# FFN norm factors formed for a quarter of the tokens per strip, and T4's low parts moved from GpSimd to VectorE, in a one-layer hybrid decoder step

## The chip, the cores and the metric

One core of one Trainium2 chip runs the whole program. The metric is the device time of one execution in microseconds. The kernel before takes 1257.67 us, the median of three runs from 1257.44 to 1259.98.

## What is computed

The reference is one layer over 16 meta tokens, 1,024 prompt tokens and 8 sequences of 4 sample tokens, width 1,024, all in fp32. A mixing part (convolution and gated delta rule) comes first, then the feed-forward part (FFN), which the change is about:

```
h = h + concat([y_a, y_b]) @ w_out
u = relu(rmsnorm(h, norm_ffn) @ w_up)         # w_up is 1024 x 4096
h = h + (u * u) @ w_down
```

`rmsnorm` multiplies each token's row by 1/sqrt(mean of squares + EPS) and each feature by a weight. The kernel multiplies by w_up first and by the token's factor afterwards, since the factor is the same for all outputs of a token.

## The kernel before

Every engine has its own list of instructions, written out by hand in program order; the engines meet by counting semaphores only. An instruction that waits holds all that stand behind it on its engine.

**Numbers.** A matmul operand is split in a high part, a rounding that TensorE takes at full pace, and a low part, the rest. A product is three matmuls for each of four blocks of 128 features: high x high, low x high, high x low (L2328, L2330, L2331, `product`), 12 in all, with 512 token columns each. ScalarE makes the high parts by a copy (L1587 for token operands, `turned_high`; L1595 for weights, `up_set_high`), and GpSimd or VectorE the low parts by a subtraction (L1158 `up_low` on GpSimd for weights; L1165 `turned_low` on GpSimd for token operands T2 and T4; L3192 `turned_low` on VectorE for T3).

**The order of products.** The 4,096 hidden features are taken in 16 pairs of 128. h is held with features in partitions and tokens in columns: 32 sample tokens, then 1,024 prompt tokens (1,056 columns in `hT`, and in `hsq`, the sums of squares). For pair 0 the four blocks of w_up are multiplied with four token operands in eight whole products, here products 1 to 8. From pair 1 on a pair takes seven products instead of eight (Strassen's scheme in Winograd's form), with sums of weight blocks (S1 to S4, made by GpSimd, L1136 to L1152) and of token blocks: B11, B21, B22 are blocks of h, T1 = B11 - B12, T3 = B12 - B22, T2 = B11 - T3, T4 = B21 - T2. A product is named here by pair and token operand. The order on TensorE is products 1 to 8, (1, B11), (1, T1), (1, B21), (1, B22), (1, T3), (1, T2), (1, T4), (2, B11), (2, T1), (2, T3), ... Raw T operands are made by VectorE (`turned_raw`, L3176, L3181, L3186) while products 1 to 8 run. Weight sets have four buffers; the high part of a set waits until the set four places earlier has been used.

**The norm factors.** After product 1 TensorE sums the squares over the partitions with a stationary operand of ones (`sum_h`, L2316): the sum of 1,056 columns is written to all 128 partitions in two matmuls, and after product 2 in a third. VectorE scales and adds EPS (`mean_h`, L3198), ScalarE takes the root of all 1,056 columns (L1639), VectorE takes reciprocals in four parts of 264 columns between its reads of later products (`root_inverse`, L3205).

**The sample tokens** go through the FFN on their own: for each two pairs TensorE runs `sample_up` (L2345, 32 small fp32 matmuls in four strips of 32 output rows, 64 records in the trace), ScalarE copies the result (`sample_copy`, L1604), TensorE transposes it (`sample_turn`, L2354), VectorE applies relu and the norm factor (`sample_scale`, L3217) and ScalarE squares it (`sample_square`, L1608). For pairs 0 and 1 `sample_up(0)` stands behind product 3 and `sample_turn(0)` behind product 7.

**VectorE** reads each finished product out of PSUM (`whole_rows`, L3277 to L3282; `up_rows`, L3241 to L3265; (1, T3) is read twice, L3244 and L3249), later scales rows of u with the factors (`scale_row1`, L3292, `scale_row0`, L3299).

**Loads.** SyncE's queue loads w_up a pair at a time into two buffers (1 MB each); the load for pair 3 waits until the low part of the weight set of (1, T4) is made.

## Time and profile before

| what | us |
|---|---|
| median of three runs | 1257.67 |
| time of the profiled execution | 1257.46 |
| its span in the trace | 1255.7 |
| TensorE (PE) busy | 1237.1, 99% |
| VectorE (DVE) busy | 801.7, 64% |
| GpSimd (POOL) busy | 646.7, 52% |
| ScalarE (ACT) busy | 462.4, 37% |

The span is that of the instructions on the engines; the execution's own time is 1.8 us longer. PE is TensorE's matmuls, PEld its weight loads, SPq the queue of SyncE. A row of a timeline gives start, duration, engine, line, operation, output <- inputs, shapes and, in brackets, how long the engine was idle before and what ended that. A matmul's duration overlaps the next one's; the distance of two starts is what it costs. The FFN begins at 580 us and its first products with w_up fill the stretch to 640 us, which the change touches.

### The profile page before, as it was taken

The page shows a single profiled execution, that of the slowest core. Times are in us where ns is not written, and L with a number is a line of the kernel's source. Part 1 is how long each engine was busy: PE and PEld are TensorE (multiplying, and loading weights), DVE is VectorE, ACT ScalarE, POOL GpSimd, SP SyncE. Part 2 cuts the span into 40 slices and gives each one's busy share as a digit, 9 for nine tenths or more (in the row PEclk, how much of TensorE's full clock was granted, in tenths as well). Part 3 has the DMA queues.
Part 4 walks back from the last instruction along what each step waited for, and adds up shares of the span by engine and source line. Part 5 has one row for each costly group of instructions (what it writes and reads, how often), then busy time and mean ns, then how long its engine had stood idle before and what let it go on. Part 6 is the DMA issues. An engine that isn't in the chain of part 4 may idle for free.

```text
span 1255.7 us, 20503 instructions
## 1 busy us (share of the span) xinstructions
PE 1237.1 (99%) x7950; PEld 1090.9 (87%) x7950; DVE 801.7 (64%) x1283; ACT 462.4 (37%) x810; POOL 646.7 (52%) x503
## 2 busy tenths in 40 slices
PE   7999999999999999999999999999999999999997
PEld 6899999899999999998778888888887888878897
DVE  6465899535564766655987685565666667556456
ACT  6565654311222222224333333333434533333312
POOL 2332120112111212213889898888789989887811
PEclk9999999999999999999999999999999999999999
DMA  6132672843323322231145353444655442541003
GB/s 205 43 85 71 176 211 72 220 123 93 93 68 85 103 68 84 79 92 52 44 158 170 121 165 136 141 143 151 226 168 202 168 140 96 201 135 68 17 10 129
DMA packets 164706, 151.07 MB, mean 120 GB/s; under 512 B 21095, under 2 KB 141315, under 8 KB 161922
## 3 DMA queue, kind: packets, MB, share of 16 engines
q1 hardware_dynamic: 141634, 136.88, 34.4%
q10 hardware_dynamic: 22976, 12.88, 3.7%
q8 instruction: 64, 1.05, 0.3%
q14 instruction: 32, 0.26, 0.1%
HBM read 103.25 MB, written 46.49 MB: 119 GB/s over the span
## 4 chain that ended last, share of the span: by engine, by line
PE 95%; DVE 2%; POOL 1%; issue 1%; DMA 1%; ACT 1%; SPq 0%; POOLq 0%; DVEq 0%; ACTq 0%
PE banks L2328 15%; PE banks L2330 15%; PE banks L2331 15%; PE banks L1792 11%; PE banks L1794 11%; PE banks L1793 11%; PE banks L2359 1%; PE banks L2345 1%; PE banks L2441 1%; PE banks L2442 1%; PE banks L2443 1%; PE banks L2262 1%; PE banks L1978 1%; DMA w_raw<-in_w_in 1%; PE banks L1971 1%
## 5 line engine op out<-in xcount | busy, mean ns | idle before, releaser
L1792 PE MATMUL banks<-xn_high,w_high 128*128 128x384 f32 (+1 forms) x672 | 227.2, 338 | 1.0 <-DVE xn_low L2565 0.9
L1794 PE MATMUL banks<-xn_high,w_low 128*128 128x384 f32 (+1 forms) x672 | 218.9, 326 | 0.0
L1793 PE MATMUL banks<-xn_low,w_high 128*128 128x384 f32 (+1 forms) x672 | 218.8, 326 | 0.0
L1002 POOL TENSOR_TENSOR w_low<-w_raw,w_high 128x1024 fp32r<-128x1024 f32 x30 | 76.8, 2559 | 230.9 <-ACT w_high L1280 230.9
L3333 DVE TENSOR_TENSOR hT<-hT,banks 128x512 f32<-128x512 f32 x148 | 98.3, 684 | 109.2 <-PE banks L2331 108.4
L1792 PEld LDWEIGHTS banks<-xn_high,w_high 128*128 128x128 f32 x672 | 127.1, 189 | 6.8 <-issue 3.6
L2328 PE MATMUL banks<-op_high,set_high 128*128 128x512 f32 x336 | 131.6, 392 | 0.0
L2330 PE MATMUL banks<-op_low,set_high 128*128 128x512 f32 x336 | 130.8, 389 | 0.0
L2331 PE MATMUL banks<-op_high,set_low 128*128 128x512 f32 x336 | 130.7, 389 | 0.0
L1793 PEld LDWEIGHTS banks<-xn_low,w_high 128*128 128x128 f32 x672 | 127.4, 190 | 0.0
L1794 PEld LDWEIGHTS banks<-xn_high,w_low 128*128 128x128 f32 x672 | 127.0, 189 | 0.0
L1158 POOL TENSOR_TENSOR set_low<-w_up_sum,set_high 128x512 fp32r<-128x512 f32 x59 | 97.4, 1656 | 28.2 <-ACT set_high L1595 28.2
L2328 PE MATMUL banks<-up_high_T,set_high 128*128 128x512 f32 x248 | 97.8, 395 | 1.8 <-POOL up_low_T L1165 1.4
L2330 PE MATMUL banks<-up_low_T,set_high 128*128 128x512 f32 x248 | 96.6, 390 | 0.0
L2331 PE MATMUL banks<-up_high_T,set_low 128*128 128x512 f32 x248 | 96.5, 389 | 0.0
L1158 POOL TENSOR_TENSOR set_low<-w_up_raw,set_high 128x512 fp32r<-128x512 f32 x49 | 77.1, 1574 | 36.7 <-ACT set_high L1595 36.6
L2328 PE MATMUL banks<-up_high_B,set_high 128*128 128x512 f32 x204 | 80.8, 396 | 0.4 <-POOL set_low L1158 0.4
L2330 PE MATMUL banks<-up_low_B,set_high 128*128 128x512 f32 x204 | 79.5, 390 | 0.0
L2331 PE MATMUL banks<-up_high_B,set_low 128*128 128x512 f32 x204 | 79.4, 389 | 0.0
L1595 ACT ACTIVATE set_high<-w_up_sum 128x512 fp32r<-128x512 f32 x59 | 37.3, 632 | 112.0 <-PE banks L2331 88.3
L2328 PEld LDWEIGHTS banks<-op_high,set_high 128*128 128x128 f32 x336 | 63.1, 188 | 15.1 <-issue 2.2
L1233 POOL TENSOR_TENSOR set_low<-w_down,set_high 128x512 fp32r<-128x512 f32 x36 | 67.2, 1873 | 16.8 <-ACT set_high L1704 16.7
(419 smaller groups left out, 2839.9 us busy)
## 6 DMA issues: line engine op xcount, KB each, us to landing
op_raw<-ops_kept SPq DMA_DIRECT2D x21, 1024.0 KB, 5.0
w_up_raw<-in_w_up SPq DMA_DIRECT2D x16, 1024.0 KB, 6.5
w_raw<-in_w_in SPq DMA_DIRECT2D x28, 512.0 KB, 4.4
ops_kept<-u_rows SPq DMA_DIRECT2D x28, 512.0 KB, 2.7
ops_kept<-u_T SPq DMA_DIRECT2D x42, 256.0 KB, 2.4
w_down_half<-in_w_down SPq DMA_DIRECT2D x3, 2048.0 KB, 9.0
w_down<-in_w_down SPq DMA_DIRECT2D x24, 256.0 KB, 4.2
w_raw<-in_w_out SPq DMA_DIRECT2D x8, 512.0 KB, 3.8
```

The costliest lines, as they stand in the source:

```text
L1002: pool.tensor_tensor(w_l[n % 2][:, :, :], w_raw[n % 2][:, :, :], w_h[n % 2][:, :, :].bitcast(F32), ALU.subtract).then_inc(w_low, 1)
L1158: pool.tensor_tensor(set_l[s % 4][:, :, :], up_source_at(s), set_h[s % 4][:, :, :].bitcast(F32), ALU.subtract).then_inc(w_low, 1)
L1233: pool.tensor_tensor(down_set(b, set_l, s), down_source(b, pair, PRODUCTS[x][0]), down_set(b, set_h, s).bitcast(F32), ALU.subtract).then_i ...
L1595: act.activation(set_h[s % 4][:, :, :], up_source(c, name), ACT.Copy).then_inc(w_high, 1)
L1792: pe.matmul(bank[:, 0:w], w_h[n % 2][:, k, :], hi[:, c0:c0 + w], start=(k == first), stop=False)
L1793: pe.matmul(bank[:, 0:w], w_h[n % 2][:, k, :], lo[:, c0:c0 + w], start=False, stop=False)
L1794: ins = pe.matmul(bank[:, 0:w], w_l[n % 2][:, k, :], hi[:, c0:c0 + w], start=False, stop=(k == last))
L1971: ins = pe.matmul(ps[5][0:c, c * h:c * h + c], kf[:, h, o:o + c], kf[:, h, o:o + c], start=True, stop=True)
L2328: pe.matmul(bank, high[:, j, :], op_high[:, j, :], start=(j == 0 and not begun), stop=False, skip_group_check=True)
L2330: pe.matmul(bank, high[:, j, :], op_low[:, j, :], start=False, stop=False, skip_group_check=True)
L2331: ins = pe.matmul(bank, low[:, j, :], op_high[:, j, :], start=False, stop=(j == n - 1), skip_group_check=True)
L3333: dve.tensor_tensor(hc, hc, both, ALU.add if sign > 0 else ALU.subtract).then_inc(acc_read_dve, 1)
```

## The change

The sums of squares are now formed by four matmuls, each over a quarter of the columns (264) and into its own strip of 32 partitions of one PSUM bank, so that [128, 264] holds all 1,056 columns. VectorE's `mean_h`, ScalarE's root and VectorE's reciprocal run once over 264 columns. `spread_h` on TensorE then writes each strip to all 128 partitions, in four banks (it sums 32 equal rows, for which `mean_h` corrects by a factor), and four ScalarE copies bring the factors back to `hsq`. `sample_up(0)` moves behind product 7 and waits for those copies, `sample_turn(0)` behind (1, T1). The low parts of T4 move from GpSimd to VectorE, and `sample_scale(0)` on VectorE moves from behind the read of (1, B21) to behind the read of (1, T3).

```diff
         A22_LOADED = [W_UP[-1] + 16 * (2 * parts_to(b) - n) for b, (_, n) in enumerate(BLOCKS)]
         A12_LOADED = [W_UP[-1] + 16 * 2 * parts_to(b) for b in range(len(BLOCKS))]
 
-        UP_HIGHS, ROOT_HIGH = {"T1": 0, "T3": (21, 22, 24, 25), "T2": (26, 27, 28, 29), "T4": (30, 31, 32, 33)}, 23
-        FIRST_HIGH, FIRST_LOW = 33, 20
-        UP_LOWS = {"B11": 7, "T1": 8, "B21": 15, "B22": 16, "T3": 20}
+        UP_HIGHS, ROOT_HIGH = {"T3": (22, 23, 24, 25), "T2": (26, 27, 28, 29), "T4": (30, 31, 32, 33)}, 21
+        FIRST_HIGH, FIRST_LOW = 33, 24
+        SPREAD_BANKS = (1, 3, 5, 7)
+        UP_LOWS = {"B11": 7, "T1": 8, "B21": 15, "B22": 16, "T3": 20, "T4": 24}
 
         def last_index(n):
             return sum(has_last(m) for m in range(n))
...
             up_low(1, 2)
             turned_low("T2", 3)
             up_low(1, 3)
-            turned_low("T4", 0)
-            turned_low("T4", 1)
             up_low(1, 5)
-            turned_low("T4", 2)
-            turned_low("T4", 3)
             for c in range(2, UP_PAIRS):
                 up_sum(c)
                 up_low(c, 0)
...
             last_half_scaled(2)
             last_half_scaled(3)
             up_set_high(0, 6)
+            act.wait_ge(rstd_mid, 1)
+            act.activation(hsq[:, 0:QUARTER], hsq[:, 0:QUARTER], ACT.Sqrt).then_inc(high_s, 1)
             turned_high("T3", 0)
             turned_high("T3", 1)
-            act.wait_ge(rstd_mid, 3)
-            act.activation(hsq[:, 0:KEPT], hsq[:, 0:KEPT], ACT.Sqrt).then_inc(high_s, 1)
+            act.wait_ge(h_sum, 2)
+            for j in range(4):
+                act.activation(hsq[:, QUARTER * j:QUARTER * j + QUARTER], ps[SPREAD_BANKS[j]][:, 0:QUARTER],
+                               ACT.Copy).then_inc(rstd_mid, 1)
+            up_set_high(1, 0)
             sample_copy(0)
-            up_set_high(1, 0)
             turned_high("T3", 2)
             turned_high("T3", 3)
             up_set_high(1, 1)
...
                     bank_free(f, g)
                     dense_part(N_IN + f, g, mixed, range(KT))
 
-            def sum_h(g):
-
-                c0, w = KEPT_GROUPS[g]
+            def sum_h():
+
                 pe.wait_ge(h_sq, 3 * N_OUT)
-                if g == 0:
-                    pe.wait_ge(x_slice_kept, 3 * N_OUT)
-                if g == 2:
-                    pe.wait_ge(rstd_mid, 1)
-                pe.matmul(ps[6 + g % 2][:, 0:w], one[:, 0:1].to_broadcast([P, P]), hsq[:, c0:c0 + w], start=True,
-                          stop=True).then_inc(h_sum, 1)
+                pe.wait_ge(x_slice_kept, 3 * N_OUT)
+                for j in range(4):
+                    ins = pe.matmul(ps[6][QUAD * j:QUAD * j + QUAD, 0:QUARTER], one[:, 0:1].to_broadcast([P, QUAD]),
+                                    hsq[:, QUARTER * j:QUARTER * j + QUARTER], start=True, stop=True)
+                ins.then_inc(h_sum, 1)
+
+            def spread_h():
+
+                pe.wait_ge(rstd_mid, 2)
+                for j in range(4):
+                    rows_ = slice(QUAD * j, QUAD * j + QUAD)
+                    ins = pe.matmul(ps[SPREAD_BANKS[j]][:, 0:QUARTER], one[rows_, 0:1].to_broadcast([QUAD, P]),
+                                    hsq[rows_, 0:QUARTER], start=True, stop=True)
+                ins.then_inc(h_sum, 1)
 
             def product(u, s, high, low, op_high, op_low, begun):
 
                 pe.wait_ge(w_low, set_made(s))
                 if u == U_UNIT[0, 4]:
-                    pe.wait_ge(rstd_mid, 3)
+                    pe.wait_ge(rstd_mid, 1)
                 else:
                     pe.wait_ge(acc_read_dve, banks_read_before(u))
                 n, bank = high.shape[1], unit_bank(u)
...
 
                 if m == 0:
                     pe.wait_ge(smp_dve, 2)
+                    pe.wait_ge(rstd_mid, 6)
                 pe.wait_ge(w_load[0], W_UP[2 * m])
                 pe.wait_ge(w_load[1], W_UP[2 * m + 1])
                 if m >= 2:
...
 
             def up(c, x):
                 u, s, name = U_UNIT[c, x], U_SET[c, x], PRODUCTS[x][1]
-                if c == 1 and name == "T3":
+                if c == 1 and name in ("T3", "T4"):
                     pe.wait_ge(low_s, UP_LOWS[name])
-                if c == 1 and name in ("T2", "T4"):
-                    pe.wait_ge(turned_low_s, 4 if name == "T2" else 8)
+                if c == 1 and name == "T2":
+                    pe.wait_ge(turned_low_s, 4)
                 product(u, s, set_h[s % 4], set_l[s % 4], up_h[name], up_l[name], x >= 4 and (c, x) != (1, 6))
 
             def down(b, x, pair):
...
             for i in range(len(WHOLE)):
                 up_whole(i)
                 if i == 0:
-                    sum_h(0)
-                    sum_h(1)
-                if i == 1:
-                    sum_h(2)
-                if i == 2:
+                    sum_h()
+                if i == 4:
+                    spread_h()
+                if i == 6:
                     sample_up(0)
-                if i == 6:
-                    sample_turn(0)
             for c, x in U_SEQ[len(WHOLE):]:
                 up(c, x)
                 if c % 2 == 0 and x == 1:
                     sample_up(c // 2)
+                if (c, x) == (1, 1):
+                    sample_turn(0)
                 if c % 2 == 0 and x == 3:
                     sample_turn(c // 2)
                 if (c, x) == (UP_PAIRS - 1, 3):
...
                 dve.tensor_tensor(up_l[name][:, j, :], up_raw[name][:, j, :], up_h[name][:, j, :].bitcast(F32),
                                   ALU.subtract).then_inc(low_s, 1)
 
-            def mean_h(g):
-                c0, w = KEPT_GROUPS[g]
-                dve.wait_ge(h_sum, g + 1)
-                dve.tensor_scalar(hsq[:, c0:c0 + w], ps[6 + g % 2][:, 0:w], 1.0 / D, EPS, ALU.mult,
+            def mean_h():
+
+                dve.wait_ge(h_sum, 1)
+                dve.tensor_scalar(hsq[:, 0:QUARTER], ps[6][:, 0:QUARTER], float(QUAD ** 2) / D, QUAD ** 2 * EPS, ALU.mult,
                                   ALU.add).then_inc(rstd_mid, 1)
 
-            def root_inverse(i):
-
-                cols = slice(QUARTER * i, QUARTER * i + QUARTER)
+            def root_inverse():
+
                 dve.wait_ge(high_s, ROOT_HIGH)
-                link(dve.reciprocal(hsq[:, cols], hsq[:, cols]))
+                dve.reciprocal(hsq[:, 0:QUARTER], hsq[:, 0:QUARTER]).then_inc(rstd_mid, 1)
 
             def sample_rows():
...
             def sample_scale(m):
 
                 dve.wait_ge(smp_turned, m + 1)
+                if m == 0:
+                    dve.wait_ge(rstd_mid, 6)
                 dve.scalar_tensor_tensor(out=sample_quad(m),
                                          in0=ps[3][:, P * (m % 2):P * (m % 2) + P].rearrange("p (j c) -> p j c", c=NS),
                                          scalar=0.0, in1=hsq[:, 0:NS].unsqueeze(1).to_broadcast([P, 4, NS]), op0=ALU.max,
...
             whole_rows(0)
             sample_rows()
             half_low("B22", N_OUT - 1, 1, 16)
-            mean_h(0)
-            mean_h(1)
+            mean_h()
             turned_raw("T3", 0)
             whole_rows(1)
-            mean_h(2)
             turned_raw("T3", 1)
             whole_rows(2)
+            root_inverse()
             turned_raw("T3", 2)
             turned_raw("T3", 3)
             whole_rows(3)
...
             turned_raw("T4", 3)
             turned_low("T3", 3)
             up_rows(1, 1)
-            root_inverse(0)
+            turned_low("T4", 0)
+            turned_low("T4", 1)
             up_rows(1, 4)
-            root_inverse(1)
+            turned_low("T4", 2)
+            up_rows(1, 6)
+            turned_low("T4", 3)
+            up_rows(1, 2)
             sample_scale(0)
-            up_rows(1, 6)
-            root_inverse(2)
-            up_rows(1, 2)
-            root_inverse(3)
             up_rows(1, 3)
             scale_row1(0)
             up_rows(1, 5)
```

On ScalarE (`u_sample_tok` is the copy of sample_up's result, `up_raw_T_75` and `up_high_T_63` are T3, `set_high_119` here the set of (1, B11), `set_high_120` that of (1, T1), `up_high_T_64` T2). Before:

```order
L1587 ACTIVATE up_high_T_63<-up_raw_T_75 128x512 [waits turned_s] x2
L1639 ACT_TABLE_LOAD
L1639 ACTIVATE h_squares<-h_squares 128x1056 [waits rstd_mid]
L1604 ACTIVATE u_sample_tok_256<-banks 128x128 [waits smp_strips]
L1595 ACTIVATE set_high_119<-w_up_raw_230 128x512 [waits acc_done,w_load1]
L1587 ACTIVATE up_high_T_63<-up_raw_T_75 128x512 [waits turned_s] x2
L1595 ACTIVATE set_high_120<-w_up_sum_232 128x512 [waits acc_done,s_made,w_load1]
L1587 ACTIVATE up_high_T_64<-up_raw_T_74 128x512 [waits turned_s] x4
```

With the change:

```order
L1634 ACT_TABLE_LOAD
L1634 ACTIVATE h_squares<-h_squares 128x264 [waits rstd_mid]
L1584 ACTIVATE up_high_T_63<-up_raw_T_75 128x512 [waits turned_s] x2
L1639 ACTIVATE h_squares<-banks 128x264 [waits h_sum]
L1639 ACTIVATE h_squares<-banks 128x264 x3
L1592 ACTIVATE set_high_119<-w_up_raw_230 128x512 [waits acc_done,w_load1]
L1601 ACTIVATE u_sample_tok_256<-banks 128x128 [waits smp_strips]
L1584 ACTIVATE up_high_T_63<-up_raw_T_75 128x512 [waits turned_s] x2
L1592 ACTIVATE set_high_120<-w_up_sum_232 128x512 [waits acc_done,s_made,w_load1]
L1584 ACTIVATE up_high_T_64<-up_raw_T_74 128x512 [waits turned_s] x4
```

The root has moved ahead of T3's first high parts, the four copies behind them, and the copy for the sample behind set (1, B11); behind it stand the same high parts as before.

On VectorE, from the read of (1, T1) to that of (1, T2) (`u_rows_249` takes the products of pair 1, `up_low_T_72` is T4, `u_sample` the sample's scaling). Before:

```order
L3244 TENSOR_TENSOR u_rows_249<-u_rows_249,banks 128x512 [waits acc_read_dve,acc_done]
L3205 RECIPROCAL h_squares<-h_squares 128x264 [waits high_s]
L3256 COPY u_rows_249<-banks 128x512 [waits acc_done,dve_step]
L3205 RECIPROCAL h_squares<-h_squares 128x264 [waits high_s]
L3217 SCALAR_TENSOR_TENSOR u_sample_253<-banks,h_squares 128x128 [waits smp_turned,dve_step]
L3265 COPY u_rows_249<-banks 128x512 [waits acc_done]
L3205 RECIPROCAL h_squares<-h_squares 128x264 [waits high_s]
L3244 TENSOR_TENSOR u_rows_249<-u_rows_249,banks 128x512 [waits acc_read_dve,acc_done,dve_step]
L3249 TENSOR_TENSOR u_rows_249<-u_rows_249,banks 128x512 [waits acc_read_dve]
L3205 RECIPROCAL h_squares<-h_squares 128x264 [waits high_s]
L3252 TENSOR_TENSOR u_rows_249<-u_rows_249,banks 128x512 [waits acc_read_dve,acc_done,dve_step]
```

With the change:

```order
L3253 TENSOR_TENSOR u_rows_249<-u_rows_249,banks 128x512 [waits acc_read_dve,acc_done]
L3200 TENSOR_TENSOR up_low_T_72<-up_raw_T_76,up_high_T_65 128x512 [waits high_s] x2
L3265 COPY u_rows_249<-banks 128x512 [waits acc_done]
L3200 TENSOR_TENSOR up_low_T_72<-up_raw_T_76,up_high_T_65 128x512 [waits high_s]
L3274 COPY u_rows_249<-banks 128x512 [waits acc_done]
L3200 TENSOR_TENSOR up_low_T_72<-up_raw_T_76,up_high_T_65 128x512 [waits high_s]
L3253 TENSOR_TENSOR u_rows_249<-u_rows_249,banks 128x512 [waits acc_read_dve,acc_done]
L3258 TENSOR_TENSOR u_rows_249<-u_rows_249,banks 128x512 [waits acc_read_dve]
L3226 SCALAR_TENSOR_TENSOR u_sample_253<-banks,h_squares 128x128 [waits rstd_mid,smp_turned]
L3261 TENSOR_TENSOR u_rows_249<-u_rows_249,banks 128x512 [waits acc_read_dve,acc_done]
```

Four reciprocals have left, four low parts of T4 have come, and the sample's scaling stands three reads later, behind both reads of (1, T3).

## Rows read from the trace of the kernel before

**Rows 1.** Table of stages: stage, length, then PE, PEld, DVE, ACT, POOL busy, clock, DMA share, GB/s.

```profile
616.00:640.00 24.00, 21.80 (x149) 16.87 (x148) 20.09 (x16) 7.10 (x12) 24.00 (x17) 1.00 0.29 101
```

**Rows 2.** Timeline of PE, 616 to 632 us: start, us, engine, line, operation, shapes, count, idle.

```profile
617.03 0.39 PE L2328 MATMUL banks<-up_high_T,set_high 128*128 128x512 f32 x1
...
622.25 0.39 PE L2331 MATMUL banks<-up_high_T,set_low 128*128 128x512 f32 x1
624.00 0.50 PE L2328 MATMUL banks<-up_high_T,set_high 128*128 128x512 f32 x1 [1.37 <-POOL up_low_T L1165]
...
627.47 0.50 PE L2328 MATMUL banks<-up_high_B,set_high 128*128 128x512 f32 x1 [0.41 <-POOL set_low L1158]
...
630.94 0.50 PE L2328 MATMUL banks<-up_high_T,set_high 128*128 128x512 f32 x1 [0.42 <-POOL set_low L1158]
```

**Rows 3.** Timeline of PE, 583 to 593 us, around the sums and sample_up(0).

```profile
583.00 1.29 PE L2316 MATMUL banks<-h_squares,one 128*128 128x288 f32 x4
...
584.36 0.39 PE L2330 MATMUL banks<-up_low_T,set_high 128*128 128x512 f32 x1
...
586.90 0.81 PE L2316 MATMUL banks<-h_squares,one 128*128 128x384 f32 x2
...
587.77 0.39 PE L2330 MATMUL banks<-up_low_B,set_high 128*128 128x512 f32 x1
...
592.62 0.40 PE L2330 MATMUL banks<-up_low_B,set_high 128*128 128x512 f32 x1
```

**Rows 4.** Timeline of PE, 150 us: four strip sums of 304 columns (8 records).

```profile
149.97 0.34 PE L1794 MATMUL banks<-xn_high,w_low 128*128 128x384 f32 x1
150.24 0.70 PE L1912 MATMUL banks<-squares,pick 128*32 128x304 f32 x8
150.87 0.50 PE L1948 MATMUL banks<-g_spread,g_pick 128*128 128x256 f32 x2
```

**Rows 5.** Timeline of ACT, 592 and 618 us.

```profile
592.42 0.28 ACT L1604 ACTIVATE u_sample_tok<-banks 128x128 f32<-128x128 f32 x1
...
593.11 1.14 ACT L1587 ACTIVATE up_high_T<-up_raw_T 128x512 fp32r<-128x512 f32 x2
...
617.91 0.31 ACT L1608 ACTIVATE u_sample<-u_sample 128x128 f32<-128x128 f32 x1 [5.40 <-DVE u_sample L3217]
618.13 1.14 ACT L1595 ACTIVATE set_high<-w_up_raw 128x512 fp32r<-128x512 f32 x2
```

**Rows 6.** Timeline of POOL, 608 to 631 us.

```profile
608.81 5.14 POOL L1165 TENSOR_TENSOR up_low_T<-up_raw_T,up_high_T 128x512 fp32r<-128x512 f32 x3
...
623.88 1.31 POOL L1136 TENSOR_TENSOR w_up_sum<-w_up_raw 128x512 f32<-128x512 f32 x1
625.12 2.30 POOL L1158 TENSOR_TENSOR set_low<-w_up_raw,set_high 128x512 fp32r<-128x512 f32 x1
...
628.62 2.27 POOL L1158 TENSOR_TENSOR set_low<-w_up_sum,set_high 128x512 fp32r<-128x512 f32 x1
```

**Rows 7.** Timeline of DVE, 613 to 622 us.

```profile
615.76 1.79 DVE L3205 RECIPROCAL h_squares<-h_squares 128x264 f32<-128x264 f32 x1
617.59 0.29 DVE L3217 SCALAR_TENSOR_TENSOR u_sample<-banks,h_squares 128x128 f32<-128x128 f32 x1
...
620.22 0.69 DVE L3244 TENSOR_TENSOR u_rows<-u_rows,banks 128x512 f32<-128x512 f32 x1
620.83 0.68 DVE L3249 TENSOR_TENSOR u_rows<-u_rows,banks 128x512 f32<-128x512 f32 x1
```

**Rows 8.** Timeline of SP, 621 us, and the page on the DMA issues.

```profile
621.51 0.37 SPq L860 DMA_DIRECT2D w_up_raw<-in_w_up  x1
...
w_up_raw<-in_w_up SPq DMA_DIRECT2D x16, 1024.0 KB, 6.5
```

**Rows 9.** Timeline of PE, 17 us, near the start of the kernel.

```profile
17.18 0.46 PE L1794 MATMUL banks<-xn_high,w_low 128*128 128x304 f32 x1
17.44 0.46 PE L1792 MATMUL banks<-xn_high,w_high 128*128 128x304 f32 x1
```

## The prediction

> **What bounds the kernel.** A product is named by its weight pair and the token operand it uses, as (1, T3). I read the table of stages first, then TensorE's timeline, then the other engines' timelines over the same microseconds. In the stage from 616 to 640 us TensorE is busy for 21.80 of 24 us at a granted clock of 1.00 [rows 1]. Before and after that stage it hardly pauses, so the end of the kernel moves by whatever TensorE loses or wins here. TensorE's timeline shows where it loses [rows 2]. A product is 12 matmuls of 512 columns, 0.23 us apart, so 2.72 us. The last matmul of (1, T2) starts at 622.25, and (1, T4) starts at 624.00 instead of 622.48: the wait is put down to GpSimd's last low part of T4. (2, B11) starts at 627.47 and (2, T1) at 630.94, each 0.4 us after it could, both for a low weight set from GpSimd. With the slower first matmul after each pause (0.35 instead of 0.23) these waits cost 3.0 us: two products from 622.48 on would have let (2, T1) start at 627.9 instead of 630.94. GpSimd is the engine behind, and the diff takes four of its instructions away. The question is whether that queue really ends earlier.
>
> **The change, part by part.**
>
> *Sums on TensorE.* The first two sums take from 583.00 to 584.13 (the second matmul of the next product starts at 584.36, 0.23 after its first would have), 1.13 us; the third from 586.90 to 587.54, 0.64 us [rows 3]. Removed: 1.77 us for 1,056 columns. Added: four sums of 264 columns into four strips of 32 output rows. The nearest rows are four such strip sums of 304 columns in the mixing part: from 150.15 (0.17 after the start at 149.97) to 150.87, 0.72 us [rows 4]. By rows 3 a column costs 1.77/1,056 us, so 304 take 0.51 and 264 take 0.44; 0.72 less 0.07, plus 0.1 for the slower restart: I take 0.75. The spread is four matmuls that each read one strip of 32 input rows and write all 128 output rows to banks of their own. No row shows input strips side by side; the lower bound is the 0.72 of rows 4, the upper the 1.77 of rows 3 (one after another). I take 0.75, because different strips and different banks leave nothing that they share. Net on TensorE: 0.75 + 0.75 - 1.77 = **-0.3 us** (+0.8 at the upper bound).
>
> *Roots and reciprocals.* VectorE loses four reciprocals of 1.79 us and gets one, and four low parts of T4 instead; ScalarE's root shrinks from 1,056 to 264 columns and four copies of PSUM are added. TensorE waits for none of it: the reciprocal is done some 2.5 us after the third product (its row is read in 0.7, then 1.79), and the spread comes only after the fifth, 5.4 us after it. This part costs and gives nothing.
>
> *The sample's products are moved, and ScalarE's queue is not.* This is the term that decides. TensorE issues sample_up(0) after product 7 instead of after product 3, since it now waits for the spread norms. ScalarE still has sample_copy(0), which waits for it, ahead of the last two high parts of T3, of set (1, T1), of all four of T2 and so on. Before, sample_up(0) ended at 592.39 (0.23 before the start at 592.62) and the copy started at 592.42 [rows 3, 5]. Now it ends four products later, less the saving on the sums, plus the spread: 592.39 + 4 x 2.72 - (1.77 - 0.75) + 0.75 = 603.0 us. ScalarE then does the copy (0.2), two high parts (1.14) and the high part of set (1, T1) (0.6): 605.0 us [rows 5]. GpSimd can begin the low part of that set at 605.0, not earlier.
>
> From there GpSimd has nine instructions up to the end of low set (1, T3) (low (1, T1), S2, low (1, B21), S4, low (1, B22), three low parts of T2, low (1, T3)), and one wait of 0.7 us, since S4 goes to ScalarE for its high part first. Their price has two ends in this trace: 1.31 where VectorE is not reading two SBUF operands, 1.71 (5.14 for three) where it is [rows 6]. Sum: 605.0 + 0.7 + 9 x 1.31 = 617.5 at the least, and with 9 x 1.71 it is 621.1 at the most. I take 1.66, near the upper end, because VectorE has the raw and low parts of T3 and T4 in just these microseconds, now four low parts of T4 more: **620.6 us**.
>
> The Trainium skill, "GPSIMD Engine Reference", section "Key points", says that GpSimd shares its SBUF interfaces with VectorE and is disturbed by VectorE's instructions with two SBUF inputs. That speaks against moving T4's subtractions to VectorE: by the rule alone all nine cost the upper price and the kernel ends at 1261.7; if it did not hold, the lower price and 1258.1. The trace agrees as far as it goes (1.71 beside such instructions, 1.31 without).
>
> TensorE is ready for (1, T3) at 617.03 - 0.3 = 616.75 [rows 2]. It waits **3.9 us**, and starts 3.6 us later than before.
>
> *sample_scale(0) moved behind (1, T3) on VectorE.* ScalarE's sample_square(0) waits for it, and the high part of set (1, T4) stands behind that square (before: square at 617.91, high part at 618.13 [rows 5]). Now: product (1, T3) ends; VectorE begins to read it 0.2 us later (a matmul lasts 0.39 and the next starts after 0.23 [rows 2]), reads it twice (0.61 each), scales (0.29), ScalarE squares (0.22 until the next begins) and makes the high part (0.6) [rows 5, 7]. With the handovers that is 2.6 us after the product's end at 620.6 + 2.8 = 623.4: 626.0. GpSimd's low set then takes 1.3 to 1.5: (1, T4) starts at 627.5, against 624.00: again **+3.5 us**. So the four instructions taken from GpSimd give nothing: the wait for T4's low part is replaced by a wait for T4's weight set, 1.4 us after (1, T2) ends at 626.1.
>
> *After that* GpSimd does S1, low (2, B11), S3, low (2, T1) as before, from 623.88 to 630.89, 7.0 us [rows 6]; now from 627.5 to 634.5. (2, T1) starts at 634.5 against 630.94. From here TensorE runs without a pause, as before, and nothing gives the time back.
>
> *DMA.* The load of weight pair 3 waits for low set (1, T4): issued at 621.51 before [rows 8], now 6 us later, 627.5; with 6.5 to land it is there at 634.0, and its first reader, sample_up(1), comes after (2, T1), at 634.5 + 2.7 = 637.2. Hidden, with 3 us to spare.
>
> **Sum.** +3.5 us. The profiled execution has a span of 1255.7 and a time of 1257.46, so 1259.2 and 1261.0; the median of the runs is 0.2 above it: **1261.2 us**. A measurement of this kernel tells from no change what is beyond 0.2%, 2.5 us: 1255.2 to 1260.2 counts as the same.
>
> **Rivals.**
>
> 1. *GpSimd catches up in part.* If its nine instructions cost 1.31 to 1.5 us, (1, T3) starts at 617.5 to 619.2, 0.5 to 2.2 later than before, and everything behind it too: 1258.1 to 1259.9. For it: VectorE's copies out of PSUM and its pauses do not slow GpSimd. Against: the three at 608.8 averaged 1.71 with less beside them. Chance 0.16.
>
> 2. *The clock falls in the new pause.* The longest pause of TensorE after its start is now 1.4 us, and the clock stays at its upper level, 2.4 GHz. A pause of 3.9 us is not in this trace. What the lower level costs is: at 17 us the matmuls of 304 columns start 0.25 apart, which is 1.2 GHz [rows 9]; by that 512 columns take 0.43 instead of 0.23, 2.4 us more for a product. If (1, T3) runs so, the end is +5.9, 1263.6; with (1, T2) too, 1 us more, since most of that is hidden by the wait for T4's set: 1264.6. Chance 0.12. The Trainium skill, "TensorE: Matmul & The Clock Gate", section "Loop structure matters more than you think", warns that waits between bursts of matmuls bring the clock down to half; only the rows at the start speak to it here.
>
> 3. *The spread's strips run one after another*: 1.77 instead of 0.75, sample_up(0) ends 1.0 later, and with it the whole chain: 1262.2. Chance 0.06.
>
> 4. *Faster.* GpSimd is relieved of four instructions of at least 1.3 us, and TensorE's 3.0 us of waits and the 0.3 of the sums come back: 1254.4. It decides itself at two points: low set (1, T3) must be done by 616.75, and the high part of set (1, T4) must be made by 620. Against: the second hangs on sample_scale(0), which is now queued behind (1, T3), and even with the first point met the chain from that product's end gives 619.5 + 2.6 + 1.4 = 623.6, 0.4 better than before, not 3. Chance 0.04.
>
> **How the numbers follow.** My forecast has 0.62, its own range 1260.4 to 1262.0. It and rivals 2 and 3 are slower by over 0.2% but for a few per cent of the forecast: 0.76. Same: rival 1 and those few, 0.20. Faster: 0.04. The range from 1258.8 to 1263.7 leaves out the faster case, the lower half of rival 1 and half of rival 2, 0.18.
>
> **What would show it.** Right: in the changed profile ScalarE idles until about 603 us for sample_up(0); GpSimd idles until about 605; TensorE pauses nearly 4 us before (1, T3), put down to a low weight set, not to a low part of T; a second pause of 1.4 us before (1, T4), again for a weight set, with ScalarE's square waiting for VectorE just ahead. Wrong: (1, T3) starts before 619; or matmuls behind the pause stand 0.43 apart; or the spread takes over 1.5 us.

## The result and the profile after

The changed kernel takes **1261.04 us**, the median of 20 runs (1258.28 to 1264.57); the kernel before, run beside it on the same chip, 1257.68 us (20 runs, 1255.54 to 1259.98). The ratio is 1.0034, 95% interval 1.0028 to 1.004: slower by 3.4 us. The profiled execution has a span of 1259.1 us and a time of 1260.87 us.

The table of stages and TensorE's timeline of the changed kernel, with the columns of [rows 1] and [rows 2]; the product's lines are now L2336, L2338 and L2339:

```profile
616.00:640.00 24.00, 19.01 (x128) 14.49 (x129) 11.92 (x13) 6.46 (x11) 19.32 (x13) 0.93 0.21 67
616.00:619.00 3.00, 0.00 (x0) 0.00 (x0) 1.81 (x3) 0.00 (x0) 3.00 (x3) 1.00 0.00 0
619.00:622.00 3.00, 2.97 (x7) 2.42 (x8) 0.00 (x0) 0.00 (x0) 2.40 (x2) 0.51 0.00 0
```

```profile
619.03 0.71 PE L2336 MATMUL banks<-up_high_T,set_high 128*128 128x512 f32 x1 [3.13 <-issue]
619.54 0.63 PE L2338 MATMUL banks<-up_low_T,set_high 128*128 128x512 f32 x1
619.97 0.63 PE L2339 MATMUL banks<-up_high_T,set_low 128*128 128x512 f32 x1
...
622.52 0.40 PE L2339 MATMUL banks<-up_high_T,set_low 128*128 128x512 f32 x1
622.76 0.40 PE L2336 MATMUL banks<-up_high_T,set_high 128*128 128x512 f32 x1
...
627.45 0.47 PE L2336 MATMUL banks<-up_high_T,set_high 128*128 128x512 f32 x1 [1.12 <-issue]
...
630.87 0.50 PE L2336 MATMUL banks<-up_high_B,set_high 128*128 128x512 f32 x1 [0.42 <-POOL set_low L1159]
...
634.34 0.50 PE L2336 MATMUL banks<-up_high_T,set_high 128*128 128x512 f32 x1 [0.41 <-POOL set_low L1159]
```

TensorE is busy for 19.01 of the 24 us instead of 21.80. It stands still for 3.13 us before (1, T3), and then the clock is down: the matmuls stand 0.43 us apart until 622.52, at a granted clock of 0.51, the lower of its two levels, 1.2 GHz. A pause of 1.12 us before (1, T4) follows, and the two pauses of 0.4 us before (2, B11) and (2, T1) are still there. "issue" as releaser means that no semaphore event of the trace falls on the end of the wait; what ended it shows on the other engines. ScalarE and GpSimd, answering to [rows 5] and [rows 6]:

```profile
595.55 0.66 ACT L1592 ACTIVATE set_high<-w_up_raw 128x512 fp32r<-128x512 f32 x1
602.00 0.28 ACT L1601 ACTIVATE u_sample_tok<-banks 128x128 f32<-128x128 f32 x1 [5.79 <-PE banks L2354]
602.18 1.14 ACT L1584 ACTIVATE up_high_T<-up_raw_T 128x512 fp32r<-128x512 f32 x2
603.22 0.62 ACT L1592 ACTIVATE set_high<-w_up_sum 128x512 fp32r<-128x512 f32 x1
...
625.17 0.31 ACT L1605 ACTIVATE u_sample<-u_sample 128x128 f32<-128x128 f32 x1 [12.49 <-DVE u_sample L3226]
625.39 1.14 ACT L1592 ACTIVATE set_high<-w_up_raw 128x512 fp32r<-128x512 f32 x2
```

```profile
603.92 1.30 POOL L1159 TENSOR_TENSOR set_low<-w_up_sum,set_high 128x512 fp32r<-128x512 f32 x1 [5.10 <-ACT set_high L1592]
...
612.15 5.11 POOL L1166 TENSOR_TENSOR up_low_T<-up_raw_T,up_high_T 128x512 fp32r<-128x512 f32 x3
617.23 1.70 POOL L1159 TENSOR_TENSOR set_low<-w_up_sum,set_high 128x512 fp32r<-128x512 f32 x1
...
626.08 1.27 POOL L1159 TENSOR_TENSOR set_low<-w_up_raw,set_high 128x512 fp32r<-128x512 f32 x1 [4.68 <-ACT set_high L1592]
```

ScalarE idles 5.79 us for sample_up(0), GpSimd 5.10 us behind it for the high part of set (1, T1); the low set of (1, T3) ends at 618.93, and TensorE starts 0.1 later. After (1, T3), ScalarE's square ends an idle time of 12.49 us, GpSimd waits 4.68 us for the high part behind it, and then TensorE gets set (1, T4).

The sums, answering to [rows 3]:

```profile
581.96 0.66 PE L2314 MATMUL banks<-h_squares,one 128*32 128x264 f32 x8
...
593.66 0.73 PE L2323 MATMUL banks<-h_squares,one 32*128 32x264 f32 x8
```

The first sum starts at 581.96 instead of 583.00. This 1.04 us does not come from the change, but from the start of the kernel, which the change does not touch. In this execution the matmuls of 304 columns stand 0.14 us apart from 15.00 on, where those of [rows 9], at 17 us, are still 0.25 apart:

```profile
14.54 0.46 PE L1793 MATMUL banks<-xn_high,w_high 128*128 128x304 f32 x1
14.79 0.37 PE L1794 MATMUL banks<-xn_low,w_high 128*128 128x304 f32 x1
15.00 0.30 PE L1795 MATMUL banks<-xn_high,w_low 128*128 128x304 f32 x1
15.14 0.30 PE L1793 MATMUL banks<-xn_high,w_high 128*128 128x304 f32 x1
```

I therefore compare stretches by one distance: from the start of the first sum to the start of sample_up(1), which stands behind (2, T1). It is 633.89 - 583.00 = 50.89 us before, and 637.28 - 581.96 = 55.32 after: **+4.43**, of which the luck at the start hides 1.04; the other 3.4 us are what the spans show.

### The profile page after: what moved, and what is told of

It is laid out like the page before. It is cut to its first block, busy times and chain, and to the rows that moved or that the text cites. A ratio compares the mean times of both kernels' runs of the same rounds, so it can differ in the third digit from the quotient of the medians.

```text
span 1259.1 us, 20517 instructions
## 1 busy us (share of the span) xinstructions
PE 1237.4 (98%) x7960; PEld 1089.8 (87%) x7960; DVE 798.0 (63%) x1282; ACT 461.7 (37%) x814; POOL 640.7 (51%) x499
## 4 chain that ended last, share of the span: by engine, by line
PE 92%; issue 3%; DVE 2%; POOL 2%; ACT 1%; DMA 1%; SPq 0%; ACTq 0%; POOLq 0%; DVEq 0%
PE banks L2336 14%; PE banks L2339 14%; PE banks L2338 14%; PE banks L1793 11%; PE banks L1795 11%; PE banks L1794 11%; PE banks L2368 1%; PE banks L2452 1%; PE banks L2450 1%; PE banks L2451 1%; PE banks L2354 1%; PE banks L2263 1%; PE banks L1979 1%; POOL set_low L1159 1%; DMA w_raw<-in_w_in 1%
## 5 line engine op out<-in xcount | busy, mean ns | idle before, releaser
L2336 PE MATMUL banks<-op_high,set_high 128*128 128x512 f32 x336 | 131.6, 392 | 0.0
L2338 PE MATMUL banks<-op_low,set_high 128*128 128x512 f32 x336 | 130.8, 389 | 0.0
L2339 PE MATMUL banks<-op_high,set_low 128*128 128x512 f32 x336 | 130.7, 389 | 0.0
L2336 PE MATMUL banks<-up_high_T,set_high 128*128 128x512 f32 x248 | 98.5, 397 | 4.7 <-issue 4.3
L2338 PE MATMUL banks<-up_low_T,set_high 128*128 128x512 f32 x248 | 97.3, 392 | 0.0
L2339 PE MATMUL banks<-up_high_T,set_low 128*128 128x512 f32 x248 | 97.0, 391 | 0.0
L2336 PE MATMUL banks<-up_high_B,set_high 128*128 128x512 f32 x204 | 80.5, 395 | 0.4 <-POOL set_low L1159 0.4
L2338 PE MATMUL banks<-up_low_B,set_high 128*128 128x512 f32 x204 | 79.5, 390 | 0.0
L2339 PE MATMUL banks<-up_high_B,set_low 128*128 128x512 f32 x204 | 79.4, 389 | 0.0
L2336 PEld LDWEIGHTS banks<-op_high,set_high 128*128 128x128 f32 x336 | 63.1, 188 | 15.0 <-issue 2.2
```

The source lines that it names most:

```text
L2336: pe.matmul(bank, high[:, j, :], op_high[:, j, :], start=(j == 0 and not begun), stop=False, skip_group_check=True)
L2338: pe.matmul(bank, high[:, j, :], op_low[:, j, :], start=False, stop=False, skip_group_check=True)
L2339: ins = pe.matmul(bank, low[:, j, :], op_high[:, j, :], start=False, stop=(j == n - 1), skip_group_check=True)
```

## The experiments

"Stretch" is that distance, as the difference to the 50.89 of before. The kernels E1 to E4 ran on one chip beside 35 runs of before (median 1257.85), E5 to E8 on another beside 29 (1258.44), E9 and E10 on a third beside 21 (1256.36), E11 and E12 on a fourth beside 19 (1260.07).

| kernel | stretch | waits of TensorE in it | median | ratio, 95% |
|---|---|---|---|---|
| before | 0 | 1.37, 0.41, 0.42 | | |
| changed, its profile | +4.43 | 3.13, 1.12, 0.42, 0.41 | 1261.04 | 1.0034, 1.0028 to 1.004 |
| E1 copy later | -0.55 | 1.12, 0.42, 0.46 | 1257.7 | 1.0002, 0.9993 to 1.0011 |
| E2 square later | 0.0 | 3.13 | 1258.99 | 1.001, 1.0 to 1.002 |
| E3 both later | -3.42 | none | 1254.68 | 0.9974, 0.9965 to 0.9983 |
| E4 T4 alone | +0.77 | 2.13 | 1258.38 | 1.0008, 1.0 to 1.0017 |
| E5 pause filled | +2.89 | 0.46, 1.12, 0.42, 0.41 | 1259.31 | 1.0006, 0.9992 to 1.002 |
| E6 changed, T4 back | +4.60 | 1.35, 4.50 | 1262.41 | 1.0023, 1.0009 to 1.0038 |
| E7 E3, T4 back | -0.23 | 1.35, 0.46, 0.42 | 1257.56 | 0.9981, 0.9967 to 0.9995 |
| E8 changed again | +2.86 | 3.13, 1.12, 0.45, 0.46 | 1261.03, one run | |
| E9 T4 alone, gaps | -1.68 | 0.92 | 1255.28 | 0.9991, 0.9982 to 1.0 |
| E10 as E3 | -3.41 | none | 1254.24 | 0.9978, 0.9969 to 0.9986 |
| E11 T4 alone, late | -2.13 | 0.78 | 1255.34 | 0.9969, 0.9954 to 0.9983 |
| E12 as E3 | -3.42 | none | 1254.54 | 0.9964, 0.9952 to 0.9976 |

**E1.** The changed kernel, with the sample's copy behind T4's second high part on ScalarE:

```diff
             up_set_high(1, 0)
-            sample_copy(0)
             turned_high("T3", 2)
...
             turned_high("T4", 1)
+            sample_copy(0)
             up_set_high(1, 6)
```

> The changed kernel with one line moved: ScalarE's sample_copy(0) stands behind the second high part of T4, ahead of set (1, B22), instead of ahead of T3's last high parts. Theory (the copy that waits for the moved sample_up(0) holds ScalarE and with it GpSimd's chain): GpSimd does low set (1, T1) right after S3, TensorE has no pause before (1, T3), no matmul there stands 0.43 apart, and only the wait before (1, T4) for its weight set stays, 1.4 us. (2, T1) starts about where it does in the kernel before: ratio to before 0.9995 to 1.000, 1257.2 us. Rival (GpSimd's nine instructions, slowed by VectorE's T4 subtractions, are late by themselves): a pause of over 1 us before (1, T3) stays, 1259 or more.

The pause before (1, T3) is gone; (1, T4) still starts 1.12 us late, and the stretch is 2.86 + 0.55 = 3.4 us shorter than that of the changed kernel (E8). Without that one line's place on ScalarE's list there is no first pause; how long the pause is depends on T4's move too, as E6 shows below. The median came out 0.5 us above the one expected.

**E2.** The changed kernel, with the square behind the second high set of pair 2 instead of ahead of the high part of set (1, T4):

```diff
-            sample_square(0)
             up_set_high(1, 5)
...
             for x in range(3):
                 up_set_high(2, x)
+                if x == 1:
+                    sample_square(0)
```

> The changed kernel with the other line moved: ScalarE's sample_square(0) stands behind the high part of set (2, T1) instead of ahead of set (1, T4). Theory (the second wait, before (1, T4), comes from sample_scale(0) behind (1, T3) and the square ahead of the high part): the pause of 3 us before (1, T3) stays with its slow matmuls, the pause before (1, T4) is gone, GpSimd starts S1 of pair 2 some 3 us earlier, the waits at (2, B11) and (2, T1) shrink to nothing: 3 us less than the changed kernel, 1257.5 to 1258.5. Rival (T4's low parts, now on VectorE, are what (1, T4) waits for): it stays at 1261.

The pause before (1, T3) stays, and nothing behind it waits any more, (2, B11) and (2, T1) included: the square's place costs 2.86 us, more than the 1.12 of its own pause, since GpSimd no longer begins pair 2 late. The median, 1258.99, is 0.5 us above the range expected and 1.1 above before, though the stretch is that of before. In the profiled execution the clock stayed up in the pause; in seven of the twelve runs the mean granted clock was lower than in any run of before on that chip (see E8).

**E3.** Both moves.

> Both lines moved. Theory: what the two moves of sample_up(0) and sample_scale(0) did through ScalarE's order is undone, and what remains is the relief of GpSimd by four instructions and 0.3 us less of sums on TensorE: no pause before (1, T3), (1, T4), (2, B11), at most 0.5 us before (2, T1): 3.3 us faster than before, 1254.2. Rival (relief is given back elsewhere, in ScalarE or VectorE): within 1 us of before.

TensorE never waits. Its windows, columns as in [rows 1]:

```profile
610.00:614.00 4.00, 4.00 (x20) 3.26 (x19) 4.00 (x4) 1.62 (x3) 4.00 (x4) 1.00 0.00 0
614.00:618.00 4.00, 4.00 (x19) 3.31 (x18) 4.00 (x5) 0.63 (x1) 4.00 (x3) 1.00 0.00 0
618.00:622.00 4.00, 4.00 (x19) 3.33 (x18) 3.66 (x6) 0.63 (x1) 4.00 (x4) 1.00 0.00 0
622.00:626.00 4.00, 4.00 (x20) 3.30 (x19) 2.77 (x3) 1.46 (x3) 4.00 (x4) 1.00 0.81 237
```

GpSimd begins low set (1, T1) at 600.84, 16.84 us behind the first sum (584.00 here), and not 21.96 behind it as in the changed kernel:

```profile
600.84 1.75 POOL L1159 TENSOR_TENSOR set_low<-w_up_sum,set_high 128x512 fp32r<-128x512 f32 x1
602.55 1.73 POOL L1141 TENSOR_TENSOR w_up_sum<-w_up_sum,w_up_raw 128x512 f32<-128x512 f32 x1
...
614.68 1.74 POOL L1159 TENSOR_TENSOR set_low<-w_up_sum,set_high 128x512 fp32r<-128x512 f32 x1
```

The time is below both kernels. **E10 and E12** are the same kernel on two more chips:

> The changed kernel with both moves on ScalarE's list (sample_copy(0) behind T4's second high part, sample_square(0) behind the second high set of pair 2), run once more on another occasion and beside the kernel that keeps the norm as it was. If the order of ScalarE's list is what the change lacked: no wait of TensorE in the stretch, 3 to 3.5 us less than before, ratio 0.9973 or so again. If the first result leant on its chip or on luck with the clock: a ratio over 0.9985.

> The changed kernel with both moves on ScalarE's list, on the same chip and in the same rounds as the kernel with the norm kept, so that the two can be compared within one occasion. Theory A: 1 us or more faster than the kernel with the norm kept. Theory B: within 0.5 us of it.

The stretch agrees to 0.01 us on all three chips, and each interval lies wholly below 1.

**E4.** The kernel before, with only T4's low parts moved to VectorE, between its four reciprocals:

```diff
             up_rows(1, 1)
+            turned_low("T4", 0)
+            turned_low("T4", 1)
             root_inverse(0)
             up_rows(1, 4)
-            root_inverse(1)
+            turned_low("T4", 2)
             sample_scale(0)
+            root_inverse(1)
             up_rows(1, 6)
+            turned_low("T4", 3)
             root_inverse(2)
```

> The kernel before with T4's low parts on VectorE, among its four reciprocals, and everything of the norm as it was. Theory: VectorE then has 4 x 0.65 to 1.7 us more in front of (1, T4), with four reciprocals of 1.79 in the same queue; (1, T4) starts about when it did, at 624, its wait now for VectorE or none, but GpSimd is ahead afterwards and the waits at (2, B11) and (2, T1) go: 1.0 to 1.5 us faster, 1256.3. Rival (VectorE cannot take them beside four whole reciprocals): (1, T4) waits for VectorE's low part and later, 1258 to 1260.

VectorE is late in GpSimd's place. A reciprocal at 619.63 holds up the read of (1, B22), whose bank (1, T2) needs. VectorE first, then TensorE:

```profile
619.63 1.79 DVE L3201 RECIPROCAL h_squares<-h_squares 128x264 f32<-128x264 f32 x1
621.46 0.69 DVE L3261 COPY u_rows<-banks 128x512 f32<-128x512 f32 x1
```

```profile
622.29 0.77 PE L2324 MATMUL banks<-up_high_T,set_high 128*128 128x512 f32 x1 [2.13 <-DVE u_rows L3261]
622.86 0.63 PE L2326 MATMUL banks<-up_low_T,set_high 128*128 128x512 f32 x1
623.28 0.63 PE L2327 MATMUL banks<-up_high_T,set_low 128*128 128x512 f32 x1
```

Here too the clock fell, after a pause of 2.13 us: (1, T2) takes 4.37 us to the next product's start instead of some 2.8, so an estimate of the stretch without the fall is 0.77 - 1.55 = -0.8. The gain expected, 1.0 to 1.5 us in the median, did not come; as the rival had it, VectorE could not take the four beside four reciprocals, but it was late with a read and not with a low part.

**E6 and E7.** T4's low parts back on GpSimd, in the changed kernel (E6) and in E3 (E7):

```diff
             up_low(1, 3)
+            turned_low("T4", 0)
+            turned_low("T4", 1)
             up_low(1, 5)
+            turned_low("T4", 2)
+            turned_low("T4", 3)
```

> The changed kernel with T4's low parts back on GpSimd, in their old places; everything of the norm and the sample's moves stays. Theory: (1, T3) starts 0.5 to 1.8 us earlier, since GpSimd's instructions before it stand beside fewer VectorE instructions with two SBUF inputs, but GpSimd has four more in front of the end: (1, T4) waits for the last low part of T4 again and starts 1 to 1.5 us later than in the changed kernel; in all 0.3 to 1 us more, 1261.5. Rival (moving T4 to VectorE is what made the changed kernel slow): 1258 or less.

> The version with both lines moved, but T4's low parts back on GpSimd: the norm part of the change alone, without its harm through ScalarE's order. Theory: the norm's part gives only the 0.3 us of the sums less 0.1, since the old waits for T4's low part at (1, T4), and for the sets of (2, B11) and (2, T1), are all back: within 0.5 us of the kernel before, 1257.5. Rival (the reciprocals taken from VectorE are worth something by themselves, GpSimd being less disturbed or banks free earlier): 1 us or more faster than before.

E6 has the longest stretch and the highest median, 0.9 us above the one expected (its ratio, 1.0023, stands beside a before of 1258.44 on that chip). GpSimd begins low set (1, T1) 21.96 us behind the first sum, as in the changed kernel, but is through with its nine instructions up to low set (1, T3) sooner:

```profile
612.67 3.79 POOL L1166 TENSOR_TENSOR up_low_T<-up_raw_T,up_high_T 128x512 fp32r<-128x512 f32 x3
616.41 1.26 POOL L1159 TENSOR_TENSOR set_low<-w_up_sum,set_high 128x512 fp32r<-128x512 f32 x1
```

These four take 5.05 us, where they take 5.11 + 1.70 = 6.81 in the changed kernel. (1, T3) starts 35.29 us behind the first sum instead of 37.07, and TensorE waits 1.35 us before it instead of 3.13. The only difference is T4's subtractions. So 1.78 us of the first pause is what they cost GpSimd when they run on VectorE, and 1.35 us is left when the copy is late and they are not there. Behind that, GpSimd has four more instructions, and TensorE waits 4.50 us for the last low part of T4 (granted clock 0.77 from 626 to 630, so the clock fell here too). (1, T4) starts 45.48 us behind the first sum, against 43.89 in E8: counted to that point, T4's move is worth 1.6 us in the late chain.

E7 has the waits of [rows 2] again and only the sums' gain: the norm's change alone is worth 0.2 us in the stretch, as expected. Its ratio, 0.9981, would be 2.4 us; the trace shows nothing of that size, and the runs of before on that chip scatter from 1255.6 to 1263.7 us, so I go by the stretch. The ratios of E11 and E12 lean on a high median of before in the same way.

**E9 and E11.** Is the norm's change needed at all? The kernel before with T4's low parts on VectorE and other places for the reciprocals. E9 fills VectorE's gap of 2.8 us before the fourth whole product's read with the first one and puts the second behind T3's second low part; E11 puts the second to fourth behind T4's last low part and the two reads after it. In both, T4's first two low parts stand behind the read of (1, T1) and the third behind that of (1, B21). The two edits in one, without the lines that are taken out:

```diff
             turned_raw("T3", 3)
+            root_inverse(0)
             whole_rows(3)
...
             turned_low("T3", 1)
+            root_inverse(1)       # E9 only
             whole_rows(7)
...
             turned_low("T4", 3)
+            root_inverse(1)       # E11; root_inverse(2) in E9
             up_rows(1, 2)
+            root_inverse(2)       # E11; root_inverse(3) in E9
             up_rows(1, 3)
+            root_inverse(3)       # E11 only
```

> The kernel before with T4's low parts on VectorE and the norm left as it was, but with two of the four reciprocals moved into earlier gaps of VectorE: the first behind the last raw part of T3, the second behind T3's second low part; sample_scale(0) behind T4's third low part. It asks whether the quartered norm is needed at all. Theory A (T4's move and the norm's change need each other because VectorE has no room for four reciprocals and four low parts): VectorE comes late with a read or a low part in this order too, TensorE waits 1 us or more for VectorE, and the time is that of the kernel before or more, 1257.5 to 1259. Theory B (only the order mattered, the room is there in the gaps): no wait of TensorE for VectorE between (1, T3) and (2, T1), sample_up(1) comes 3.4 to 3.7 us earlier, as with the good order of the changed kernel, 1254.0 to 1254.9. In between, 1255 to 1257: the early reciprocals hold up T3's low parts or GpSimd a little.

> As the run before it with the norm kept as it was and T4's low parts on VectorE, but the second reciprocal, behind which the read of (1, B11) came late there (TensorE waited 0.92 us before (1, B21)), stands behind T4's last low part, and the third and fourth one read later each. VectorE has its gap of 2.8 us filled by the first reciprocal only. Theory A (VectorE has no room for four reciprocals in this stretch wherever they stand; the quartered norm is needed for the full gain): a new wait for VectorE turns up, at (1, T4) or at pair 2, and sample_up(1) comes at most 2 us earlier than before, 1255.5 or more. Theory B (it was the place alone): no wait, sample_up(1) 3.0 us earlier (the whole of the waits of before, without the 0.1 to 0.4 of the sums), 1254.5 to 1255.1; then the norm's change is worth only its 0.1 to 0.4 us of sums.

Each leaves one wait for a late read of VectorE, 0.92 us before (1, B21) in E9 and 0.78 us before (2, T1) in E11:

```profile
629.48 0.47 PE L2324 MATMUL banks<-up_high_T,set_high 128*128 128x512 f32 x1 [0.78 <-DVE u_rows L3259]
```

Both stretches are shorter than that of before, though E9's ratio reaches 1.0 and E11's leans on a slow before. E10 and E12, beside them, are quicker still: stretches of -3.4 against -1.7 and -2.1, medians 1.0 and 0.8 us lower. Both results lie between what the two theories expected: a wait for VectorE is there (theory A), but part of the gain comes without the norm's change (theory B). In the two orders tried VectorE had no room for all four reciprocals; that no order has it is not shown.

**E5 and E8.** E8 is the changed kernel once more. E5 puts 12 matmuls of 512 columns into the pause, behind (1, B22), that write a bank nobody reads before it is overwritten:

```diff
+                if (c, x) == (1, 6):
+                    for j in range(12):
+                        pe.matmul(ps[7][:, :], up_h["B22"][:, 0, 0:P], up_h["B22"][:, j % 4, :], start=True, stop=True)
```

> The changed kernel with 12 more matmuls of 512 columns into a PSUM bank that nobody reads, between (1, B22) and (1, T3), so that TensorE works through 2.7 of the 3.1 us in which it waits; the rest is unchanged. Theory (in the changed kernel's profile the clock fell to its lower level in the pause and cost 1.5 us on (1, T3)): (1, T3) starts at the same distance from the FFN's begin, its matmuls stand 0.23 apart, (1, T4) and all behind it come up to 1.5 us earlier than in that profile; in the median over runs 0.5 to 1.5 us less than the changed kernel, 1259.6 to 1260.5, and its runs scatter less. Rival (the slow matmuls have another cause, such as GpSimd or loads): they stay slow and the time is 1261 or, with the added work, more.

> The changed kernel once more, one look with a profile. Theory: the pause of 3.1 us before (1, T3) is there again to 0.1 us, and whether the clock falls in it is open, since it did here and not in the same pause with the square moved; if it doesn't, the stretch is 1.5 us shorter. Rival (the fall belongs to the changed kernel): the matmuls of (1, T3) stand 0.43 apart again.

The stretch of E8 is +2.86, not +4.43, with the same pauses. Its windows show why:

```profile
616.00:619.00 3.00, 1.65 (x8) 1.03 (x6) 3.00 (x5) 0.00 (x0) 3.00 (x3) 1.00 0.00 0
619.00:622.00 3.00, 1.22 (x5) 1.05 (x6) 0.56 (x1) 0.00 (x0) 3.00 (x4) 1.00 0.00 0
622.00:625.00 3.00, 3.00 (x15) 2.48 (x14) 1.20 (x2) 0.00 (x0) 1.17 (x1) 1.00 0.00 0
```

The clock stayed at its upper level, 2.4 GHz. So the changed kernel's two late lines leave it 2.86 us behind before in an execution in which the clock stays up, and 1.57 us further behind in one in which it falls in the pause.

How often it falls there in the timed runs is not known; their mean granted clocks give a hint. A mean of 0.996 or less was found in this many runs:

| chip | kernels without a pause over 1.4 us | kernels with one (its length) |
|---|---|---|
| result | | changed 8 of 20 (3.13) |
| E1 to E4 | before 0 of 35, E1 0 of 12, E3 1 of 12 | E2 7 of 12 (3.13), E4 7 of 11 (2.13) |
| E5 to E8 | before 10 of 29, E5 0 of 12, E7 0 of 12 | E6 8 of 12 (4.50), E8 0 of 1 (3.13) |
| E9, E10 | before 0 of 21, E9 2 of 11, E10 1 of 11 | |
| E11, E12 | before 8 of 19, E11 4 of 9, E12 1 of 11 | |

The eight of the changed kernel are its slowest runs, 1261.61 to 1264.57, and on the chip of E1 to E4 the low means go with the long pauses. But the mean does not single out this fall. The profiled executions of the changed kernel and of E4 have the fall in the stretch and a mean of 0.997; that of E11 has 0.996 and no fall in the stretch, but one at 57 us and one at 1248. E8 has a fall at 57 us too, where the change is not yet at work:

```profile
57.00:58.00 1.00, 1.00 (x5) 1.00 (x5) 0.66 (x3) 0.97 (x2) 0.20 (x2) 0.50 0.00 0
```

Falls like these may be what lowers the mean of before on two of the chips; no trace of such a run of before was taken.

E5's stretch of +2.89 is that of E8, so filling the pause could only gain in executions where the clock falls. None of its 12 runs was at 0.996 or less, and its median, 1259.31, lies 0.3 us below the range expected, but its ratio, 1.0006 with an interval of 0.003, can't be set against that of the changed kernel, which was timed on another chip: what the filling saves on the median stays open.

## Why the prediction was right

Times are moved by +1.04 (changed kernel) or by -0.71 (E8), so that the first sum starts at 583.00.

- *Sums.* Forecast 0.75; measured 581.87 to 582.65, 0.78. Spread: forecast 0.75, measured 0.85 (593.58 to 594.43). Four strips of 32 input rows do run beside each other, and **rival 3 falls**. Net -0.14 instead of -0.3, of no account.
- *sample_up(0) ends* at 603.0 (forecast 603.0); *low set (1, T1) starts* at 604.96 (605.0). This was the step that decides, and E1 shows that without it there is no first pause.
- *GpSimd's nine instructions* took 14.2 us, 1.58 each; I took 1.66. The low set of (1, T3) was done at 619.97 instead of 620.6, and TensorE paused 3.13 instead of 3.9 us. This is the term that was mis-sized, by 0.7 us: the first two instructions cost the lower price, 1.30. VectorE is idle beside the first until 604.9; beside most of the second it makes a raw part from two SBUF inputs, and there it is VectorE's instruction that is slow, 1.50 instead of 0.74. **Rival 1**, at 1.5 or less, is out, though by little: in E6, without T4's subtractions on VectorE, the nine took 12.4 us, 1.38 each, which lies in its range. The rule of the Trainium skill that I weighed ("GPSIMD Engine Reference", "Key points": GpSimd and VectorE share SBUF interfaces) would have had all nine at 1.71. The trace agrees with it for the other seven, which took 1.5 to 1.75, and E6 agrees with what I took from it against T4's move (1.78 us); the second instruction, at 1.30, does not agree. The upper price that I read, 1.71, is also not the highest of [rows 6]: a low set there takes 2.30. None of the nine met that price.
- *sample_scale(0) behind (1, T3)*: from that product's end to the start of (1, T4) 4.0 us, forecast 4.1. In E8 (1, T4) starts at 626.9, forecast 627.5, and the 0.6 between them is GpSimd's. E2 shows the square as the cause.
- *Pair 2*: GpSimd needs 7.0 us, as forecast. (2, T1) is at 633.8 in E8, forecast 634.5, so the forecast of +3.5 was **+2.86** without the clock.
- *The load* of pair 3 was issued at 628.4 (forecast 627.5), and sample_up(1) did not wait for it.
- **Rival 2**, the clock falling in the pause, came true in the profiled execution and was absent in E8. Its price was 1.6 us, not the 2.4 of a whole product, because the clock was back after the eighth matmul. I gave it 0.12; the traces show it in one of the two executions of this kernel. It is no rival but an addition, which some executions have: the mechanism forecast for the pause is there with it and without it.
- *The four instructions taken from GpSimd.* That they give nothing holds against before, where the wait for T4's weight set takes the place of the wait for T4's low part. It does not hold within the late chain: without the move (E6) (1, T4) starts 1.6 us later still.
- **Rival 4**, faster: the 3 us that I named are there. E3 takes them, with two lines moved. About its second point, the chain behind sample_scale(0), I was right: with the copy alone moved (E1) the gain is 0.55 us, and I had put it at 0.4.

That the forecast of 1261.2 comes within 0.2 us of the median of 1261.04 is partly luck. The terms that the forecast is made of give +2.86 and not +3.5. In the profile the fall of the clock adds 1.57 to that, and the earlier start takes off 1.04; in E8 there is no fall, and a first sum 0.71 us later than that of before's profile brings its one run to 1261.03. The median of 20 runs holds a mix of such executions.

What the change set out to do needs all its parts. T4's move alone makes VectorE late (E4; with better places a part of the gain, E9 and E11), the norm's change alone gains its sums (E7), and together they gain 3.4 us, if ScalarE's list lets GpSimd begin in time (E3).

## What to carry to other kernels

When a step is moved later on one engine, move the instructions that wait for it on every other engine too. What counts is not the moved step, but what is queued behind its consumer and feeds the engine that was the late one. Look for such an instruction by its idle time: ScalarE was busy 37% of the span, and one copy of 0.2 us at the wrong place on its list cost 3.4 us at the end (E8 against E1). And a relief of one engine by another has to be paid for in the other's timeline, gap by gap, around the reads that free the banks.

## What was not expected of the hardware

- The clock is not a function of the pause alone. After the same pause of 3.13 us the granted clock was 0.51 in one execution and 1.00 in two (E8, E2), and in E4 it fell after only 2.13 us (0.57 from 622 to 626). In the changed kernel's profile the fall cost 1.57 us, eight matmuls at 0.43 us instead of 0.23.
- It also fell where TensorE had no pause. In E1, E8 and E11 it was at 0.50 at 58 us, though the trace shows TensorE busy throughout from 50 us on, at 54 to 56 us with small matmuls (16x8). In E8 the matmuls of 304 columns stand 0.25 us apart there, as at the start of the kernel. Between 19 and 583 us E8 loses 1.5 us against the changed kernel's other execution, which has no such fall.
- At the start of the kernel TensorE's pace had risen by 15.0 us in one execution and not yet at 17.4 in another. This moves the whole program by 1 us and is no effect of the change. The granted clock in the profile reads 1.00 there in both, so only the distance of the matmuls shows it. With both effects the first sum lies anywhere from 581.27 (E10) to 584.00 (E3) in the 14 traces (these two are the same kernel); spans of single profiles should be compared from a mark behind it.
- One subtraction of 128 x 512 on GpSimd costs 1.29 or 1.74, and one on VectorE 0.68 or 1.78, with values between, by what the other does; beside VectorE's scaling of 1,024 columns one on GpSimd took 2.3. In E3 GpSimd had 1.74 from 600.84 to 621.5 nearly throughout, and the kernel still gained: the contention that T4's move brought was 1.8 us (E6), the later start of GpSimd's chain 5.1 us.
